# A chunked recurrence on one core: products per head and a dense state instead of products per head pair

## The chip, the cores and the metric
The kernel runs on one core of a Trainium2 chip. The metric is device time in microseconds (us) of one execution. Three runs of the kernel before took 1755.32, 1756.28 and 1759.92 us (median 1756.28). The profile is one further execution; its own time and its span stand below.

## The reference, cut to what matters
The program computes two blocks in float32, for 512 tokens of width 1024. The first block has a mixer whose left half is a recurrence over tokens in 8 heads of width 64, and whose right half is a causal convolution of 31 taps followed by a layer norm over 512 channels:

```
def step(S, inp):
    r_t, w_t, k_t, v_t, a_t, b_t = inp
    sa = jnp.einsum("bhvk,bhk->bhv", S, a_t)
    S = S * w_t[:, :, None, :] + sa[..., None] * b_t[:, :, None, :] + v_t[..., None] * k_t[:, :, None, :]
    y = jnp.einsum("bhvk,bhk->bhv", S, r_t)
    return S, y
...
y = _head_group_norm(y, lnx_g, lnx_b)
...
c = jax.nn.silu(_layer_norm(_causal_dwconv(c, cconv_w, cconv_b), cln_g, cln_b))
mix = jnp.concatenate([rwkv_out, c], axis=-1) @ w_out
```

The initial S is zero. The rest of the first block (a gated feed-forward with a short convolution) and the second block (two attention layers with modulation vectors from `silu(c) @ ada_w + ada_b`) are not touched.

## The kernel before, in words
Activations lie transposed, channels on the 128 partitions and tokens along the free dimension. 512 channels of the recurrence are 4 tiles (`CT`) of 128, each with two heads: head e of a pair has partitions 64e to 64e+63. Large products run as three products of split values (`w_hi`, `w_lo`); GpSimd (POOL) makes the split of each 1 MB weight block in `split`, 4 quarters of two operations. One instruction queue per engine is written out by hand, in order; engines meet by semaphores, and all loads are issued in order by SyncE (SP).

The recurrence has three stages.

1. The units, before about 304 us. For each pair c and head e, `unit` on TensorE, ScalarE (ACT) and VectorE (DVE) inverts a triangular matrix per chunk of 64 tokens and makes from it `eA` (step W), `U` (step U), `RBt` and the part `ky` of the output that needs no state. In the same stage ACT and POOL compute most of the convolution's taps: ACT writes a scaled tap to one of four buffers, POOL adds it to `cacc` (line 670, 96 additions), and `conv_done` counts them. Two of those buffers lie where `SA` and the second state buffer lie.
2. The chain over 8 chunks (`for n in range(NCH)`, TensorE lines 918 to 965, DVE lines 2328 on). The state `St` holds a 128x128 matrix for each pair, with zeros in the two blocks off the diagonal; DVE clears both buffers first (line 2322), after it has waited for the last tap. A chunk is: the products `eA` times state (line 926) for SA; `SA = product + U` on DVE (line 2332); the products of the state with `eR` (line 933); the products of B with SA and of K with V for the next state, 64x128 operands (lines 939, 940); per head SA with `RBt` (line 944) for the output; on DVE the old state times its decay (line 2337, two operations), then eight operations that add the product times the decay to the diagonal blocks (line 2345); and the output added to `ky` (line 2363).
 Beside the chunks stand: the products of the modulation vectors, one 1 MB block of `ada_w` after chunks 0, 2, 3, 5 and 6 (`CHAIN_ADA`, line 771, each 32 products); the convolution's mean in four 128x512 products after chunk 1 (line 950), centring on DVE (line 2351), squares on ACT, their sum in 32-partition blocks after chunk 4 (line 958), the root on ACT, its reciprocal on DVE and its spreading after chunk 5 (line 964), and the normalization on DVE (line 2361).
3. The group norm of `ky` (line 991 on), gating on POOL (line 682), and the output projection (lines 977 to 979), whose first tiles take the convolution's half.

SP's order in this stretch: two blocks of `ada_w`; the first output weight block once TensorE has read modulation block 0; the second once it has read block 1; then the third after the first is split; then further `ada_w` and weight blocks. POOL's order: additions of taps; splits of output blocks 0, 1 and 2; gating of the bonus (line 678); gating by `ky` (line 682); split of block 3.

Of the kernel before, what the change touches and what calls it, by code (L numbers as in the profile page):

```python
# [23 lines left out]
P = 128  # L24
# [90 lines left out]
def build(nc, x_t, ctx_t, stream, ada_w, vectors, squares, level_masks, scan_mask, ropes, lora_w, gate_w,  # L115
# [92 lines left out]
    St = [reg("St0", [P, CT, P], 143), reg("St1", [P, CT, P], 90)]  # L208
# [71 lines left out]
    ACT_STEPS = ["LT", "DIT", "MV", "Y0", "G1", "G2", "G3", "G4", "G5", "W", "U"]  # L280
    DVE_STEPS = ["MT", "RB", "RK", "DT0", "D0"] + [s + str(n) for n in range(1, 5) for s in "PT"] + ["Q5"]
# [14 lines left out]
    st_zero = sem("st_zero")  # L296
# [136 lines left out]
    kpe_copied = Later(sa_full, NCH)  # L433
    kpe_turned = Later(sa_done, NCH)
# [3 lines left out]
    mla_filled = Later(st_done, 2 * (NCH - 1))  # L438
# [49 lines left out]
    lam_exp = Later(cln_root, 3)  # L488
# [48 lines left out]
    def _(sp):  # L537
# [40 lines left out]
        ada_block(4, 2)  # L578
        weights(out0 + 3, out0 + 4)
        ada_block(5, 3)  # L580
        sp.wait_ge(y_done, NCH)
        sp.wait_ge(cln_sum, 1 + CT)
# [51 lines left out]
    def _(pool):  # L634
# [40 lines left out]
        split(out0 + 2, half_of(out0 + 2), out0 // 2 + 1, done=out0, to=0, hi=w3_hi, lo=w3_lo)  # L675
# [3 lines left out]
        for c in range(CT):  # L679
            pool.wait_ge(gn_centred, c + 1)  # L680
            pool.wait_ge(*bonus_gated.at(c + 1))
            pool.tensor_tensor(gg[:, c, :], gg[:, c, :], ky[:, c, :], ALU.mult).then_inc(y_gated.sem, 1)
        split(out0 + 3, half_of(out0 + 3), (out0 + 3) // 2, done=out0, to=0, hi=w4_hi, lo=w4_lo)
# [35 lines left out]
    def _(pe):  # L719
# [195 lines left out]
        CHAIN_ADA = {0: 1, 2: 2, 3: 3, 5: 4, 6: 5}  # L915
        pe.wait_ge(st_zero, 1)
        for e in range(2):
            pe.wait_ge(u_act[e], act_at(CT - 1, "U"))
        for n in range(NCH):
            tt, r = n // 2, slice(64 * (n % 2), 64 * (n % 2) + 64)  # L920
            t0 = CHUNK * n
            state = St[n % 2]
            if n:
                pe.wait_ge(st_done, 2 * n)
            for c in range(CT):
                mm = pe.matmul(banks[0][r, P * c:P * c + P], eA[:, c, t0:t0 + CHUNK], state[:, c, :], start=True, stop=True)
            mm.then_inc(sa_full, 1)
            if n >= 2:
                pe.wait_ge(y_done, n - 1)
            yb = banks[2 + n % 2]  # L930

            for c in range(CT):
                pe.matmul(yb[:, CHUNK * c:CHUNK * c + CHUNK], state[:, c, :], eR[:, c, t0:t0 + CHUNK], start=(c == 0), stop=False,
                          skip_group_check=True)
            pe.wait_ge(sa_done, n + 1)
            if n < NCH - 1:
                for c in range(CT):
                    ch = slice(P * c, P * c + P)
                    pe.matmul(banks[1][:, ch], B_tok[r, tt, ch], SA[r, ch], start=(c == 0), stop=False, skip_group_check=True)
                    mm = pe.matmul(banks[1][:, ch], K_tok[r, tt, ch], V_tok[r, tt, ch], start=False, stop=(c == CT - 1), skip_group_check=True)  # L940
                mm.then_inc(st_full, 1)
            for h in range(8):
                c, hr = h // 2, slice(64 * (h % 2), 64 * (h % 2) + 64)
                mm = pe.matmul(yb[hr, CHUNK * c:CHUNK * c + CHUNK], SA[r, 64 * h:64 * h + 64],
                               RBt[h][r, tt, 64 * (n % 2):64 * (n % 2) + 64], start=False, stop=(h == 7), skip_group_check=True)
            mm.then_inc(y_full, 1)
            if n == 1:
                pe.wait_ge(conv_done, len(ADDED))
# [1174 lines left out]
    def _(dve):  # L2123
# [197 lines left out]
        for st in St:  # L2321
            last = dve.memset(st[:, :, :], 0.0)
# [799 lines left out]
```

## Time and profile before
| | |
|---|---|
| median of 3 runs | 1756.28 us |
| the profiled execution's own time | 1760.59 us |
| its span | 1758.8 us |
| TensorE busy | 1679.9 us (96%) |
| VectorE / ScalarE / GpSimd busy | 1008.4 / 759.2 / 953.3 us |

### The profile page before, as it was taken

The numbers are of one execution on the slowest core, as the hardware profiler recorded it, in microseconds if no ns is written. First come the engines' busy times: TensorE is split into PE (matmuls) and PEld (weight loads), VectorE is DVE, ScalarE is ACT, GpSimd is POOL, SyncE is SP. The second block draws the span as 40 slices with busy tenths as digits, with TensorE's granted clock in tenths as the row PEclk, the third lists the DMA queues.
The fourth block names the chain that finished last, engine by engine and source line by source line (L and its number), as shares of the span: only waits on it lengthen the run. The fifth ranks groups of instructions, "written<-read, shape, count | busy, mean of one in ns | idle before, by whom it ended". The sixth has DMA issues, their size and how long they took to land.

```text
span 1758.8 us, 26144 instructions
## 1 busy us (share of the span) xinstructions
PE 1679.9 (96%) x10282; PEld 1368.5 (78%) x10282; DVE 1008.4 (57%) x1276; ACT 759.2 (43%) x1253; POOL 953.3 (54%) x758
## 2 busy tenths in 40 slices
PE   8999999988899999998998999999989999999887
PEld 7677998766588888887887777776877888888775
DVE  4698564574655555003346566676575666666575
ACT  4552888022333333003223655656134444444562
POOL 4444899734399999998446032034634444444062
PEclk9999999699899999999999999999989999999998
DMA  5221000433022222434112000002231111111211
GB/s 193 72 96 48 2 1 18 177 121 120 25 95 95 95 95 95 168 113 163 49 48 72 1 25 15 11 0 77 91 157 49 49 48 49 48 49 48 92 53 48
DMA packets 18867, 126.33 MB, mean 72 GB/s; under 512 B 2096, under 2 KB 2352, under 8 KB 4304
## 3 DMA queue, kind: packets, MB, share of 16 engines
q1 hardware_dynamic: 18624, 124.41, 19.3%
q8 instruction: 72, 1.18, 0.3%
q10 hardware_dynamic: 144, 0.52, 0.1%
q14 instruction: 27, 0.22, 0.0%
HBM read 122.83 MB, written 2.10 MB: 71 GB/s over the span
## 4 chain that ended last, share of the span: by engine, by line
PE 53%; issue 18%; POOL 16%; DVE 9%; ACT 3%; DMA 0%; POOLq 0%; ACTq 0%; DVEq 0%; SPq 0%
POOL w_hi L648 8%; PE banks L1227 5%; POOL cacc L670 4%; PE banks L1206 4%; POOL w_lo L639 3%; PE banks L1384 3%; PE banks L1387 3%; PE banks L1385 3%; PE banks L1089 3%; PE banks L1094 3%; PE banks L1090 3%; PE banks L751 2%; PE banks L1439 2%; PE banks L752 2%; PE banks L753 2%
## 5 line engine op out<-in xcount | busy, mean ns | idle before, releaser
L648 POOL TENSOR_TENSOR w_hi<-raw,der 128x512 fp32r<-128x512 f32 x296 | 340.8, 1162 | 454.4 <-PE banks L1387 186.9
L639 POOL TENSOR_TENSOR w_lo<-raw,w_hi 128x512 fp32r<-128x512 f32 x336 | 468.5, 1406 | 66.2 <-ACT w_hi L1530 66.2
L751 PE MATMUL banks<-h_hi,w_hi 128*128 128x512 f32 x496 | 198.5, 400 | 5.6 <-DVE h_lo L2369 5.3
L752 PE MATMUL banks<-h_lo,w_hi 128*128 128x512 f32 x496 | 194.1, 391 | 0.0
L753 PE MATMUL banks<-h_hi,w_lo 128*128 128x512 f32 x496 | 193.9, 391 | 0.0
L1384 PE MATMUL banks<-h_hi,w_hi 128*128 128x512 f32 (+1 forms) x384 | 146.4, 381 | 1.2 <-DVE h_lo L2685 1.0
L1385 PE MATMUL banks<-h_lo,w_hi 128*128 128x512 f32 (+1 forms) x384 | 131.5, 357 | 2.3 <-issue 2.3
L2014 ACT ACTIVATE dP<-banks,der 128x768 f32<-128x768 f32 x64 | 57.7, 902 | 160.2 <-DVE der L2773 160.2
L751 PEld LDWEIGHTS banks<-h_hi,w_hi 128*128 128x128 f32 x496 | 93.5, 188 | 35.2 <-issue 12.7
L1387 PE MATMUL banks<-h_hi,w_lo 128*128 128x512 f32 (+1 forms) x384 | 116.4, 357 | 0.0
L698 POOL TENSOR_TENSOR Of<-Of,Ls 128x768 f32<-128x768 f32 x8 | 14.7, 1832 | 186.7 <-DVE Ls L2575 186.7
L752 PEld LDWEIGHTS banks<-h_lo,w_hi 128*128 128x128 f32 x496 | 93.7, 189 | 19.9 <-issue 1.4
L753 PEld LDWEIGHTS banks<-h_hi,w_lo 128*128 128x128 f32 x496 | 93.7, 189 | 19.7
L2773 DVE TENSOR_REDUCE der<-banks 128x1 f32<-128x768 f32 x64 | 60.7, 953 | 68.3 <-PE banks L1420 68.3
L1227 PE MATMUL banks<-Pf,V 128*128 128x512 f32 x192 | 98.9, 596 | 0.3 <-issue 0.3
L1089 PE MATMUL banks<-h_hi,w_hi 128*128 128x512 f32 (+1 forms) x256 | 92.0, 359 | 5.1 <-DVE h_lo L2472 2.3
L2564 DVE TENSOR_REDUCE nmr<-banks 128x1 fp32r<-128x768 f32 x64 | 60.5, 945 | 59.7 <-PE banks L1177 58.9
L1867 ACT ACTIVATE Pf<-banks 128x512 f32<-128x512 f32 x112 | 66.6, 595 | 62.7 <-PE banks L1206 60.9
L1384 PEld LDWEIGHTS banks<-h_hi,w_hi 128*128 128x128 f32 x384 | 72.7, 189 | 18.1 <-DVE h_lo L2685 2.3
L1090 PE MATMUL banks<-h_lo,w_hi 128*128 128x512 f32 (+1 forms) x256 | 85.3, 350 | 0.0
L1385 PEld LDWEIGHTS banks<-h_lo,w_hi 128*128 128x128 f32 x384 | 73.0, 190 | 13.0 <-issue 4.7
L670 POOL TENSOR_TENSOR cacc<-glu_s,cacc 128x512 f32<-128x512 f32 x48 | 60.6, 1286 | 34.5 <-ACT glu_s L1628 34.5
(490 smaller groups left out, 4095.8 us busy)
## 6 DMA issues: line engine op xcount, KB each, us to landing
raw<-in_stream SPq DMA_DIRECT2D x84, 1024.0 KB, 4.8
ada_raw<-in_ada_w SPq DMA_DIRECT2D x18, 1024.0 KB, 7.0
raw<-in_ada_w SPq DMA_DIRECT2D x4, 1024.0 KB, 5.0
xT<-in_x_t SPq DMA_DIRECT2D x2, 1024.0 KB, 6.0
xT<-in_x_t SPq DMA_DIRECT2D x1, 2048.0 KB, 7.7
ada_end<-in_ada_w SPq DMA_DIRECT2D x2, 1024.0 KB, 6.0
out_t<-z SPq DMA_DIRECT2D x8, 256.0 KB, 2.1
ctxT<-in_ctx_t SPq DMA_DIRECT2D x1, 1024.0 KB, 7.2
```

The lines of the kernel that those rows point to most:

```text
L639: return pool.tensor_tensor(lo[:, h, part(i), :], raw_tiles(half)[:, part(i), :], hi[:, h, part(i), :], ALU.subtract)
L648: pool.tensor_tensor(hi[:, h, part(i), :], raw_tiles(half)[:, part(i), :], one, ALU.mult).then_inc(hi_done, 1)
L670: pool.tensor_tensor(cacc[:, j, :], tap_out[i % 4], cacc[:, j, :], ALU.add).then_inc(conv_done, 1)
L751: pe.matmul(banks[b][:, :], hi, tile(rhs_hi, k), start=(at_k == 0), stop=False)
L752: pe.matmul(banks[b][:, :], hi, tile(rhs_lo, k), start=False, stop=False)
L753: mm = pe.matmul(banks[b][:, :], lo, tile(rhs_hi, k), start=False, stop=(at_k == KT - 1))
L1089: pe.matmul(out, hi, cols(rhs_hi, k0 + k, a, b), start=(k == 0), stop=False)
L1090: pe.matmul(out, hi, cols(rhs_lo, k0 + k, a, b), start=False, stop=False)
L1227: mm = pe.matmul(pairs[1][:, 0, :], v[:, j, :], Pf[:, i % 4, :], start=(j == 0), stop=(j == 5), skip_group_check=True)
L1384: pe.matmul(out, hi, h2_hi[:, k, a:b], start=(k == 0), stop=False)
L1385: pe.matmul(out, hi, h2_lo[:, k, a:b], start=False, stop=False)
L1387: mm = pe.matmul(out, lo, h2_hi[:, k, a:b], start=False, stop=(k == KT - 1))
```

## The change
- The state becomes dense: two buffers `state` of 128 x 4 x 64 without the zero blocks, and all products of the chain are made per head with 64x64 operands, the two heads of a pair in different rows or columns of TensorE.
- The decay of a chunk is put into `eA` and `eR` in the units: on DVE, step W (which was on ACT) multiplies while it copies, and one more operation per pair scales `eR`. The old state times its decay goes to ACT (`keep_state`, four operations of 128x64 for each chunk from 1 to 6, into `kept`), and DVE then makes the next state in one addition of 128x256.
- Chunk 0 has no products with the state: SA is `U`, the next state is a copy, the buffers are not cleared, and the wait for the last tap stands before SA of chunk 1.
- The mean of the convolution is summed in 32-partition blocks (`conv_sums`) and spread (`conv_spread`), as the squares were; the pieces of that layer norm are placed one by one behind SA and behind the output in DVE's order. ACT loads the square root's table before the chain.
- Output accumulates in one bank per head half and is added in two operations of 64x256. Modulation block 1 stands behind chunk 1. POOL splits output block 2 after the gatings instead of before them; SP loads `ada` block 5 before output block 3.

```
-            for c in range(CT):
-                mm = pe.matmul(banks[0][r, P * c:P * c + P], eA[:, c, t0:t0 + CHUNK], state[:, c, :], start=True, stop=True)
+                for c, e, h, cc_ in HEADS:
+                    mm = pe.matmul(pairs[SA_PAIR][r, e, cc_], eA[HEAD[e], c, ts], kv[HEAD[e], c, :], start=True, stop=True)
...
+                for c, e, h, cc_ in HEADS:
+                    pe.matmul(banks[STATE_BANK][HEAD[e], cc_], K_tok[r, tt, h], V_tok[r, tt, h], start=(c == 0), stop=False, skip_group_check=True)
+            if n:
+                pe.wait_ge(y_done, n)
+                for c, e, h, cc_ in HEADS:
+                    mm = pe.matmul(banks[Y_BANK[e]][HEAD[e], cc_], kv[HEAD[e], c, :], eR[HEAD[e], c, ts], start=(c == 0), stop=False, skip_group_check=True)
+                mm.then_inc(y_begun.sem, 1)
+                if n == 1:
+                    pe.wait_ge(conv_done, len(ADDED))
+                    conv_sums(cacc)
+                if n == 2:
+                    conv_spread(1)
+                if n == 6:
+                    conv_spread(4)
+                pe.wait_ge(sa_done, n)
+            if n < NCH - 1:
+                for c, e, h, cc_ in HEADS:
+                    mm = pe.matmul(banks[STATE_BANK][HEAD[e], cc_], B_tok[r, tt, h], sa[r, h], start=False, stop=(c == CT - 1), skip_group_check=True)
+                mm.then_inc(st_full, 1)
+            for c, e, h, cc_ in HEADS:
+                mm = pe.matmul(banks[Y_BANK[e]][HEAD[e], cc_], sa[r, h], RBt[2 * c + e][r, tt, 64 * (n % 2):64 * (n % 2) + 64],
+                               start=(n == 0 and c == 0), stop=(c == CT - 1), skip_group_check=True)
             mm.then_inc(y_full, 1)
...
+        def keep_state(n):
+            act.wait_ge(st_done, n)
+            for c in range(CT):
+                ins = act.activation(kept[:, c, :], state[n % 2][:, c, :], ACT.Copy, scale=der[:, ECT + NCH * c + n:ECT + NCH * c + n + 1])
+            ins.then_inc(state_kept, 1)
...
+            if step == "W":
+                if e:
+                    decayed(eR[:, c, :], eR[:, c, :], slice(0, P))
+                dve.wait_ge(u_pe[e], pe_at(c, "W"))
+                decayed(eA[HEAD[e], c, :], X[0][HEAD[e], :], HEAD[e]).then_inc(u_dve[e], 1)
...
-                for e in range(2):
-                    hr = slice(64 * e, 64 * e + 64)
-                    for c in range(CT):
-                        ins = dve.scalar_tensor_tensor(out=kept, in0=banks[1][hr, P * c + 64 * e:P * c + 64 * e + 64], ...)
+                if n:
+                    dve.wait_ge(state_kept, n)
+                    dve.tensor_tensor(after, banks[STATE_BANK][:, 0:256], kept[:, :, :].rearrange("p c v -> p (c v)"), ALU.add).then_inc(st_done, 1)
+                else:
+                    dve.tensor_copy(after, banks[STATE_BANK][:, 0:256]).then_inc(st_done, 1)
```

Behind SA, DVE centres tiles 1 and 3 in chunks 3 and 4, adds modulation columns in chunk 5, normalizes tile 0 in chunk 6 and tiles 2 and 3 in chunk 7; behind the output it centres tiles 0 and 2 in chunks 2 and 3, adds modulation columns in chunk 4, inverts the root in chunk 5 and normalizes tile 1 in chunk 6. ACT's queue has squares of the centred tiles between `keep_state(2)` and `keep_state(5)`, each behind DVE's centring.

## Rows read from the trace of the kernel before

**Rows 1.** Page, part 1: busy time, share of span and instructions by engine.
```profile
PE 1679.9 (96%) x10282; PEld 1368.5 (78%) x10282; DVE 1008.4 (57%) x1276; ACT 759.2 (43%) x1253; POOL 953.3 (54%) x758
```

**Rows 2.** Windows: stretch, its length, busy by engine, PEclk, DMA share, GB/s.
```profile
176.00:304.00 128.00, 126.47 (x1159) 120.34 (x1161) 73.12 (x112) 105.55 (x184) 115.52 (x94) 1.00 0.01 2
...
308.80:319.20 10.40, 10.40 (x112) 9.45 (x112) 3.85 (x16) 0.00 (x0) 4.73 (x5) 0.50 0.48 200
319.20:333.70 14.50, 14.50 (x60) 10.14 (x56) 5.71 (x14) 0.00 (x0) 13.78 (x13) 0.54 0.43 146
...
308.80:373.56 64.76, 59.10 (x736) 49.91 (x737) 37.95 (x104) 9.43 (x14) 32.60 (x28) 0.79 0.31 114
```

**Rows 3.** Chain of waits, 300 to 382 us: start, length, what.
```profile
306.28 1.27 POOL cacc L670
...
308.80 1.97 PE banks L926 x8
...
327.84 5.96 PE banks L950 x8
...
373.56 5.33 PE banks L991 x8
```

**Rows 4.** Timeline, 290 to 345 us, TensorE: start, length, engine, line, operands.
```profile
303.88 0.94 PEld L771 LDWEIGHTS banks<-raw,sq_c 128*32 128x32 f32 x64
...
316.30 0.93 PEld L944 LDWEIGHTS banks<-RBt,SA 64*64 64x64 f32 x16 [0.22 <-issue]
316.31 1.12 PE L944 MATMUL banks<-RBt,SA 64*64 64x64 f32 x16
...
317.35 1.69 PEld L771 LDWEIGHTS banks<-raw,sq_c 128*32 128x32 f32 x64
...
337.77 0.54 PEld L944 LDWEIGHTS banks<-RBt,SA 64*64 64x64 f32 x16
```

**Rows 5.** Timeline, 345 to 402 us, TensorE.
```profile
353.20 0.81 PEld L958 LDWEIGHTS banks<-csq,sq_c 128*32 128x32 f32 x32
...
361.64 0.97 PEld L964 LDWEIGHTS banks<-crs,der 128*128 128x128 f32 x8 [1.45 <-DVE crs L2357]
```

**Rows 6.** Groups by line, 308.80 to 373.56 us: busy, mean ns, idle before.
```profile
L2345 DVE SCALAR_TENSOR_TENSOR St<-banks,der,St 64x64 f32<-64x64 f32 x56 | 12.3, 281 | 12.4 <-PE banks L940 12.0
...
L2332 DVE TENSOR_TENSOR SA<-banks,U 64x512 f32<-64x512 f32 x8 | 5.5, 688 | 12.8 <-PE banks L926 12.7
...
L2363 DVE TENSOR_TENSOR Q<-banks,Q 128x256 f32<-128x256 f32 x8 | 3.4, 421 | 0.9 <-PE banks L944 0.8
...
L2351 DVE SCALAR_TENSOR_TENSOR cacc<-banks,cacc 128x512 f32<-128x512 f32 x4 | 2.5, 682 | 0.0
...
L2357 DVE RECIPROCAL crs<-crs 128x128 f32<-128x128 f32 x1 | 1.0, 953 | 0.0
...
L1680 ACT ACTIVATE crs<-banks,der 128x128 f32<-128x128 f32 x1 | 0.4, 367 | 10.1 <-PE banks L958 10.1
```

**Rows 7.** Timeline, 264 to 280 us, DVE between two pairs of units.
```profile
274.07 1.29 DVE L2284 TENSOR_TENSOR Gt<-banks,sq_c 128x512 f32<-128x512 f32 x2 [5.30 <-PE banks L904]
```

**Rows 8.** Timeline, POOL and SP: first and second output block, third block's load.
```profile
314.47 2.04 POOL L648 TENSOR_TENSOR w_hi<-raw,der 128x512 fp32r<-128x512 f32 x2 [6.92 <-DMA raw<-in_stream]
...
323.61 0.33 SPq L547 DMA_DIRECT2D raw<-in_stream  x1
```

**Rows 9.** Timeline, 386 to 462 us, POOL.
```profile
404.34 2.22 POOL L648 TENSOR_TENSOR w_hi<-raw,der 128x512 fp32r<-128x512 f32 x2 [11.86 <-PE banks L979]
```

**Rows 10.** Timeline, 386 to 470 us, DVE: beside POOL's split, and without.
```profile
389.82 1.51 DVE L2394 TENSOR_TENSOR Q<-Q 128x512 f32<-128x512 f32 x1
...
394.33 0.69 DVE L2394 TENSOR_TENSOR Q<-Q 128x512 f32<-128x512 f32 x1
```

**Rows 11.** Line 944 alone: shortest, median, longest ns of one instruction.
```profile
L944 PE MATMUL banks<-RBt,SA x128: 218/218/363, 316.3 to 372.8; 64*64 64x64 f32 x128
```

**Rows 12.** DMA issues, whole execution: count, KB each, median us to landing.
```profile
ada_raw<-in_ada_w SPq DMA_DIRECT2D x18, 1024.0 KB, 7.0
```

More of the change, by code:

```diff
@@ L207, in build @@
     SA = reg("SA", [P, HALF], 88)
-    St = [reg("St0", [P, CT, P], 143), reg("St1", [P, CT, P], 90)]
+    state = [reg(f"state{i}", [P, CT, 64], 32 + i) for i in range(2)]
+    kept = reg("kept", [P, CT, 64], 34)
     sqk = reg("sqk", [P, 2, T], 101)
@@ L914, in _, with conv_sums @@
         ada_blocks([0])
-        CHAIN_ADA = {0: 1, 2: 2, 3: 3, 5: 4, 6: 5}
-        pe.wait_ge(st_zero, 1)
+        CHAIN_ADA = {1: 1, 2: 2, 3: 3, 5: 4, 6: 5}
         for e in range(2):
             pe.wait_ge(u_act[e], act_at(CT - 1, "U"))
+            pe.wait_ge(u_dve[e], dve_at(CT - 1, "W"))
+        def conv_sums(src):
+            for c in range(CT):
+                for j in range(4):
+                    mm = pe.matmul(banks[CONV_BANK][32 * j:32 * j + 32, 0:P], ones[:, 0:32], src[:, c, P * j:P * j + P], start=(c == 0),
+                                   stop=(c == CT - 1))
+            mm.then_inc(cln_sum, 1)
@@ L919, in _, with conv_spread @@
+        def conv_spread(done):
+            pe.wait_ge(cln_root, done)
+            for j in range(4):
+                mm = pe.matmul(banks[CONV_BANK][:, P * j:P * j + P], der[:, ROOT + j:ROOT + j + 1].broadcast_to([P, P]), crs[:, :], start=True, stop=True)
+            mm.then_inc(cln_root, 1)
+        HEADS = [(c, e, slice(64 * (2 * c + e), 64 * (2 * c + e) + 64), slice(64 * c, 64 * c + 64)) for c in range(CT) for e in range(2)]
         for n in range(NCH):
-            tt, r = n // 2, slice(64 * (n % 2), 64 * (n % 2) + 64)
@@ L942, in _ @@
[L942 to L945, printed above, removed]
-            mm.then_inc(y_full, 1)
-            if n == 1:
-                pe.wait_ge(conv_done, len(ADDED))
-                for c in range(CT):
-                    mm = pe.matmul(banks[4][:, :], ones, cacc[:, c, :], start=(c == 0), stop=(c == CT - 1))
-                mm.then_inc(cln_sum, 1)
+                pe.wait_ge(st_done, n)
@@ L954, in _ @@
             if n == 4:
[L955 to L965 removed]
+                pe.wait_ge(cln_sq, CT)
+                conv_sums(csq)
         pe.wait_ge(y_done, NCH)
@@ L1654, in unit @@
                 out, src = Gt[e][:, :, :], X[0][:, :]
-            elif step == "W":
-                out, src = eA[rows, c, :], X[0][rows, :]
             else:
@@ L2319, in _ @@
                     unit(c, e, step)
-        dve.wait_ge(conv_done, len(ADDED))
-        for st in St:
-            last = dve.memset(st[:, :, :], 0.0)
-        last.then_inc(st_zero, 1)
         chain.link(dve.memset(der[:, ROOT:ROOT + 4], 0.0))
@@ new lines, in norm_conv, with by_head, behind_sa @@
+        def norm_conv(c):
+            dve.wait_ge(cln_root, 5)
+            dve.tensor_tensor(cacc[:, c, :], cacc[:, c, :], banks[CONV_BANK][:, :], ALU.mult).then_inc(cln_normed, 1)
+        def by_head(t):
+            return t.rearrange("p (c e v) -> p e c v", c=CT, e=2)
+        def behind_sa(n):
+            if n == 3:
+                centre_conv(1)
+            elif n == 4:
+                centre_conv(3)
+            elif n == 5:
+                ada_columns(1)
+            elif n == 6:
+                norm_conv(0)
+            elif n == 7:
+                norm_conv(2)
+                norm_conv(3)
@@ L2368, in low @@
+            dve.wait_ge(y_full, n + 1)
+            for e in range(2):
+                ins = dve.tensor_tensor(ky[HEAD[e], :, ts], banks[Y_BANK[e]][HEAD[e], 0:256].rearrange("p (c t) -> p c t", c=CT),
+                                        ky[HEAD[e], :, ts], ALU.add)
+            ins.then_inc(y_done, 1)
+            behind_y(n)
         def low(k, src, ready):
```

149 lines of the change are left out of this document (75 added, 74 removed).

## The prediction
> **What bounds the kernel now.** I read the page's busy times first, then the windows around the change, then the chain of waits in them, then the timeline. TensorE is busy for 96% of the span [rows 1], so time leaves mainly where it has nothing better to do. The recurrence's chain is such a place: 308.80 to 373.56 us, 64.8 us, and no engine is at its peak in it [rows 2]. The chain of waits runs there through POOL's last tap (ends 307.55), then the small matmuls from 308.80, the convolution's mean (5.96 us) and DVE, until the group norm's first product at 373.56 [rows 3]. Three things make it long. The granted clock is 0.50 in 308.8 to 319.2 and 0.54 in 319.2 to 333.7, so at the 1.2 GHz level for nearly 25 of the 65 us, though TensorE is recorded busy throughout [rows 2]. Operands are twice as wide as needed. And DVE makes the next state in eight operations of 281 ns [rows 6]. The units in front (176 to 304 us) are another matter: TensorE is busy 126.5 of 128 us [rows 2].
>
> **The units.** DVE gets, per pair, two operations from the bank (64x512, priced as line 2332: 0.69 us) and one of 128x512 (as line 2351: 0.68) [rows 6]: 2.06 us. DVE idles 5.30 us at just that place, between the last placement of one pair and the first product of the next [rows 7]. Cost 0. Bounds: if the broadcast factor doubled them to 4.1 us they would still fit; without the cover four pairs would cost 8 us. ACT loses two copies per pair, and TensorE, the bound, waited for neither: gain 0, at most 1 us. POOL's taps keep their pace.
>
> **Where the chain starts.** Before, DVE waits for the last tap, clears two buffers, and TensorE starts at 308.80. After, chunk 0 needs neither: TensorE goes on behind modulation block 0, whose weight loads run 303.88 to 304.82, and begins at about 305.0 [rows 3, 4]. Gain 3.8 us; the tap's end at 307.55 meets chunk 1's SA, which comes no earlier than 308.
>
> **The price of a group.** All products are now like line 944: 8 heads, 16 instructions of 64x64. Its loads take 0.93 us at the low clock and 0.54 at the high one; the last result is 0.19 behind [rows 4]. Different row/column placements are not shown in the trace; I bound a group by 0.3 us (half, if neighbours in different quarters overlap more) and, above, by 16 times the 218 ns that one instruction lasts [rows 11], 3.5 us, and take the row itself, since its placement is that of three of the five groups. The tiling page of the Trainium skill (TensorEngine Tiling (Array Packing), "Key Properties") says that different tiles can load and multiply in parallel; at a quarter of the price each the groups would be worth some 20 us more than I count, but line 944 already alternates tiles and shows its price.
>
> **One chunk.** There are five groups: SA, K with V, state with eR, B with SA, SA with RBt.
> - Low clock: 5 x 0.93 = 4.65 us. TensorE is the longer side: SA's addition (0.69) lies beside two groups, and the state's addition (0.42, as line 2363 [rows 6]) beside the last.
> - High clock: three groups 1.62; the fourth 0.54 + 0.14; the state 0.42 and two handovers 0.12; sum 2.84. SA on DVE (0.69) starts after the output's two additions of the chunk before (2 x 0.42; the two ends meet at 0.9 us into the chunk) and ends at 1.6, just in time.
> - ACT's four copies per chunk at about 0.3 to 0.37 each (line 1680 reads 128x128 in 0.37 [rows 6]) make 1.2 to 1.5 us, beside 2.4 us of path. In chunks 3 and 4 they stand behind a square of 0.6 that waits for DVE's centring: 0.3 us lost each. If these copies took twice as long, six chunks would lose 0.5 to 1 each; hence 5 us in the upper end.
>
> **What stands beside the chunks.** A modulation block takes 0.94 us high and 1.69 low [rows 4], as before in five chunks; it is paid after the last group, less what DVE has to do there. Sums in 32-partition blocks take 0.81 high [rows 5], I take 1.6 low. They replace the mean of 5.96 us. Spreading takes 0.97 high [rows 5] and 1.8 low, now twice instead of once. Behind the output DVE has the inverse of 0.95 and a centring of 0.68 [rows 6]; behind SA a piece of 0.68 is hidden by the fourth group.
>
> **The sum.** The clock decides, and no row shows it for this sequence. Before, small products at the low level for 19 us did not raise it, the dense 128x512 mean was followed by the high one, and small products after that mostly kept it [rows 2, 3, 4]. The change enters at the high level and without the pause of 3.8 us, but with emptier operands and no dense stretch. I take the low level for chunks 0 to 3 and the high one for 4 to 7, near the middle:
> chunk 0: three groups, 2.8; chunk 1: 4.65 + 1.6 + 1.7 = 7.95; chunk 2: 4.65 + 1.8 + 1.7 = 8.15; chunk 3: 4.65 + 1.7 = 6.35; chunk 4: 2.84 + 0.3 + 0.85 = 4.0; chunk 5: 2.84 + 0.8 (columns) + 0.95 = 4.6, the block beside it; chunk 6: spreading 0.4 beyond SA's addition, block 0.95, normalizing 0.6: 4.75; chunk 7: SA 0.68 + 0.75, two normalizations 1.36, output 0.96: 3.75. Together 42.3; the chain ends at 305.0 + 42.3 = 347.3 instead of 373.56: 26.2 us earlier.
>
> **What is late next.** POOL: output block 0 lands at 314.47 and is split until 323.6 as before, when SP issues block 2 [rows 8]; block 1 follows until about 333, the bonus until 338.5. All is before 347. Splitting block 2 now comes after the gatings: about 347.3 + 8.6 to + 18.5, block 3 to + 28. TensorE turns to block 2's tiles where POOL in the old trace found block 0's weights released, 404.34, so + 30.8 [rows 9]. Covered by 12 us; without cover 10 us. Loads: SP issues `ada` blocks 4 and 5 behind output block 2 (323.6); with the median landing of 7.0 us [rows 12] they are there at about 331 and 335, and chunks 5 and 6 want them at 339 and 344. At the high clock throughout they would be late. Group norm and projection follow the chain and move with it. But POOL's split now runs on beside DVE's last gatings: an operation that takes 0.69 alone took 1.51 beside POOL [rows 10]. Five of them, with slack in three: 1 us, bounds 0 and 3.
>
> Net 25.2 us. The profiled execution's own time is 1760.59 (span 1758.8, with 1.8 around it); 1760.59 - 25.2 = 1735.4. The median of the runs is 4.3 lower, 1756.28, so I say 1731.
>
> **Rivals.**
> 1. The clock stays high from start to end. Chunk 0 then takes 1.7 instead of 2.8, chunks 1 to 3 12.9 instead of 22.45 (2.84 each, 1.6 for the sums and spreading beyond SA's addition, blocks and centring), 10.6 less. But chunk 5 asks for its modulation block at 326 and it lands at 331, so 5 go back: end at 341.7, net 30.8, time 1725. For it: no pause before the chain. Against: the drop to 0.50 at 308.8, and TensorE recorded busy at that level until 327.8 [rows 2, 3]. The Trainium skill (TensorE: Matmul & The Clock Gate, "What's actually happening") says that activity releases the throttle; by it this is the case to expect, but the trace disagrees as far as busy time counts as activity: 10.4 of 10.4 us busy at 0.50.
> 2. The clock stays low to the end. Chunks 4 to 7 take 6.4, 6.35, 8.15 and 4.3 instead of 17.1: 8.1 more, net 17, time 1739. For it: quarter-filled products, and nothing dense any more.
> 3. The chain shortens but the gain is handed back behind it: the projection waits for POOL's later split, or for loads that SP holds back. It needs both covers above to fail, 12 us and more: net 10 or less, time 1748.
> 4. Slower: the 64x64 groups do not overlap. If two heads in the same bank or quarter had to wait for each other, an instruction would cost up to its own 218 ns [rows 11]. There are 36 groups x 16 = 576; my sum counts some 45 ns of pace each. Break-even is 25.2 us over 576, 44 ns more, so a pace of about 90 ns; at 218 ns the chain is 100 us longer. At 130, midway: + 49, less 25: 1780. Against it: line 944 runs at 34 to 58 ns a piece with alternating output halves.
> That the change doesn't do what it says I see no room for: each old group is gone from the text.
>
> **Chances.** Forecast (1731, own range 1727 to 1736) 0.46; all low 0.25; all high 0.17; handed back 0.08; slower 0.04. The range must reach the first two rivals and the copies on ACT: 1721 to 1745. A measurement of this kernel tells 0.3%, 5 us, from no change. Faster 0.93, same 0.03, slower 0.04.
>
> **What would show it.** After: line 2332's successor 0.69 us, the new state one operation of 0.42, SA groups at 0.54 or 0.93; the granted clock per chunk decides between forecast and rivals 1 and 2. TensorE's first chain product right behind modulation block 0 at about 305; the group norm's first product at 347, and from there to the first projection tile still 8.6 us. Unit stage still 128 us. I am wrong if a group takes over 1 us at the high clock, if ACT's copies end after the fourth group, or if TensorE idles before block 2's tiles.

## The result and the profile after

| | before | after |
|---|---|---|
| median of the runs | 1756.32 us (1755.32 to 1759.92) | 1732.66 us (1730.67 to 1739.2) |
| ratio, 95% interval | | 0.9868 [0.9838, 0.9898] |
| profiled execution's own time | 1760.59 us | 1731.96 us |
| its span | 1758.8 us | 1730.2 us |
| group norm's first product | 373.56 us | 344.78 us |
| first projection tile | 382.21 us | 353.49 us |
| end of the convolution's half of the projection | 429.22 us | 401.18 us |

The forecast was 1731. The two traces differ by 28.6 us, the medians by 23.7. The first trace of before was an execution 4.3 us above its median, and a second trace of the same kernel (run before_again, 1758.14) has the group norm at 372.5 instead of 373.56. There the chain also begins 2.6 us later than in the first trace (311.42 for 308.80), so it lasts 61.1 us against 64.8. In the traces of all versions below, what follows the end of the convolution's half lasts 1326.7 to 1332.2 us, though the code is the same there. What follows therefore reads places and lengths from traces and the size of a gain from medians.

Part 1 of the page after, which answers to [rows 1]: TensorE is busy 28.9 us less, about the whole of the gain in the trace.
```profile
PE 1651.0 (95%) x10522; PEld 1345.9 (78%) x10522; DVE 1004.5 (58%) x1230; ACT 760.9 (44%) x1271; POOL 958.0 (55%) x758
```

The windows of the changed kernel, with the columns of [rows 2]: the unit stage, chunks 1 and 2, chunk 5, chunk 6, the group norm, and last the whole chain.
```profile
176.00:303.50 127.50, 125.96 (x1148) 119.96 (x1145) 82.14 (x128) 100.08 (x175) 118.01 (x94) 1.00 0.01 2
...
306.20:312.10 5.90, 4.91 (x176) 4.37 (x176) 2.81 (x6) 5.27 (x15) 0.99 (x1) 1.00 0.99 407
312.10:317.30 5.20, 4.97 (x159) 4.47 (x152) 1.95 (x4) 0.00 (x0) 2.04 (x3) 1.00 0.87 320
...
325.70:334.80 9.10, 4.61 (x148) 4.21 (x144) 5.77 (x9) 2.85 (x7) 9.10 (x9) 0.83 0.89 349
334.80:341.20 6.40, 6.40 (x156) 6.00 (x152) 2.58 (x6) 0.81 (x1) 3.22 (x3) 0.71 0.37 150
...
344.78:353.49 8.71, 7.84 (x16) 2.45 (x16) 6.51 (x9) 5.69 (x10) 5.90 (x5) 0.80 0.89 346
...
304.54:344.78 40.24, 31.87 (x983) 28.87 (x977) 23.56 (x44) 17.88 (x43) 25.26 (x22) 0.92 0.57 214
```
The chain takes 40.24 us against 64.76. The clock column is the surprise: 1.00 where [rows 2] had 0.50 and 0.54, and then a fall of its own in chunks 5 and 6. Chunk 5 shows why: 9.10 us long, with TensorE busy for only 4.61 of them.

The chain of waits of the changed kernel (start, length, what) names what stood there.
```profile
305.01 10.18 DMA raw<-in_stream
...
324.62 8.20 DMA ada_raw<-in_ada_w
...
332.96 1.93 PE banks L775 x64
...
344.78 5.40 PE banks L1004 x8
```
Where [rows 3] had the convolution's mean on the path, it now goes through two loads: an output weight block, whose split (begun at 315.26) lets SP issue the next blocks, then modulation block 4, issued at 324.6. The timeline of the changed kernel shows the same place from TensorE's side, with the chain's first group and, last, POOL's split of output block 4.
```profile
304.54 0.54 PEld L949 LDWEIGHTS banks<-V_tok,K_tok 64*64 64x64 f32 x16
...
324.62 1.56 SPq L557 DMA_DIRECT2D ada_raw<-in_ada_w  x2
...
332.93 1.72 PEld L775 LDWEIGHTS banks<-ada_raw,sq_c 128*32 128x32 f32 x64 [3.67 <-issue]
332.96 1.93 PE L775 MATMUL banks<-ada_raw,sq_c 128*32 128x64 f32 x64 [3.56 <-DMA ada_raw<-in_ada_w]
...
376.31 2.22 POOL L652 TENSOR_TENSOR w_hi<-raw,der 128x512 fp32r<-128x512 f32 x2 [0.76 <-PE banks L992]
```
TensorE stands for 3.56 us, and after that the weight loads of this block take 1.72 us instead of the 0.94 of [rows 4]. Before, the landings of 7.0 us [rows 12] were hidden.

The groups by line in the chain of the changed kernel (mean ns of one, then idle before), which answer to [rows 6]:
```profile
L1691 ACT ACTIVATE kept<-state,der 128x64 f32<-128x64 f32 x24 | 6.3, 335 | 4.6 <-DVE state L2425 4.6
...
L2417 DVE TENSOR_TENSOR SA<-banks,U 64x512 f32<-64x512 f32 x7 | 4.8, 690 | 6.6 <-PE banks L945 6.1 <-POOL cacc L674 0.2
...
L2425 DVE TENSOR_TENSOR state<-banks,kept 128x256 f32<-128x256 f32 x6 | 2.5, 425 | 5.0 <-PE banks L966 4.9
...
L2430 DVE TENSOR_TENSOR Q<-banks,Q 64x256 f32<-64x256 f32 x16 | 6.7, 421 | 0.8 <-PE banks L971 0.5
```
Eight additions of 281 ns are one of 425, and the last tap (POOL, line 674) costs SA only 0.2 us.

### The profile page after: what moved, and what is told of

The parts are those of the page before. It is cut to its first block, busy times and chain, and to the rows that moved or that the text cites. A ratio compares the mean times of both kernels' runs of the same rounds, so it can differ in the third digit from the quotient of the medians.

```text
span 1730.2 us, 26591 instructions
## 1 busy us (share of the span) xinstructions
PE 1651.0 (95%) x10522; PEld 1345.9 (78%) x10522; DVE 1004.5 (58%) x1230; ACT 760.9 (44%) x1271; POOL 958.0 (55%) x758
## 4 chain that ended last, share of the span: by engine, by line
PE 56%; issue 16%; POOL 12%; DVE 9%; ACT 5%; DMA 1%; POOLq 0%; SPq 0%; ACTq 0%; DVEq 0%
POOL w_hi L652 9%; PE banks L1240 5%; PE banks L903 4%; POOL w_lo L643 4%; PE banks L1219 4%; PE banks L1397 3%; PE banks L1400 3%; PE banks L1398 3%; PE banks L1102 3%; PE banks L1107 3%; PE banks L1103 3%; PE banks L755 2%; PE banks L1452 2%; PE banks L756 2%; PE banks L757 2%
```

## The experiments

"Changed kernel" is the one after. Each is compared with before on its own chip; kernels of one set share their runs of before. The first theory: the changed chain ran at the high clock because it begins without a pause, and a large part of what that brought went back in the wait for modulation block 4 and the clock's fall behind it. Three sets follow. All differences are between medians, unless a trace is named.

### The first set: clock, load, state addition

**again**: the changed kernel once more, as the yardstick of this set.

> The changed kernel once more, unaltered, so that its profiled execution can be compared with its timed runs. Theory: the change is worth what the chain of the recurrence lost, 28.8 us in the two traces (group norm's first product at 344.78 instead of 373.56), and the median of the runs differs by less (23.7 us) because the executions differ in the clock they are granted in the chain. Then the median lies at 1731 to 1734 and the trace again starts the group norm at 343 to 348. Rival: some us are given back behind the chain in the timed runs; then the trace would show the group norm at 345 but a span above 1735.

Measured: 1730.68 (1730.4 to 1735.9), 0.9853 [0.9834, 0.9872]. Group norm at 344.7, a wait of 2.86 us for the same block: the chain's length, the wait and the fall behind it are confirmed. The clock's course is not the same, though. Windows of again:
```profile
316.00:320.00 4.00, 3.12 (x102) 2.88 (x103) 1.55 (x4) 0.90 (x3) 4.00 (x5) 0.74 0.15 59
320.00:324.00 4.00, 4.00 (x143) 3.84 (x142) 3.23 (x6) 1.32 (x4) 4.00 (x4) 0.84 0.02 4
```
It is at the low level from 318 to 321 as well, behind a halt of 1.33 us in TensorE's issue that ends at 316.88 and that was 0.23 us long in the first trace. The fourth chunk ends 1.9 us later than there, and the wait for the load takes most of that in.

**load_first**: SP issues modulation blocks 4 and 5 before the third output weight block.
```
         weights_behind(out0 + 1, 1)
-        weights(out0 + 2, out0 + 3)
         ada_block(4, 2)
         ada_block(5, 3)
+        weights(out0 + 2, out0 + 3)
```

> Modulation blocks 4 and 5 are loaded before output block 2 instead of behind it. Theory: TensorE's wait of 3.56 us at 329.4 to 332.96 is for a load that stood in the queue behind another, and the fall of the granted clock right after it (0.71 in 334.8 to 341.2) is a result of the wait. Then both go: block 4 is there before 325, the chain ends at 338 to 340 instead of 344.8, and the time falls by 5 to 6 us against the changed kernel. Rival: the low clock comes from the small products themselves; then only the wait goes, 2.5 to 3.5 us (VectorE's reciprocal ends at 331.9), and the clock falls in the same stretch.

Measured: 1726.36 (1726.2 to 1729.8), 0.9825 [0.9808, 0.9842], 4.3 less than again. Group norm at 340.5, 4.2 earlier. Windows of load_first, columns as above:
```profile
325.00:331.00 6.00, 6.00 (x152) 5.42 (x148) 3.91 (x8) 1.43 (x5) 6.00 (x7) 0.72 0.66 251
331.00:340.50 9.50, 7.76 (x269) 6.91 (x265) 8.64 (x16) 5.32 (x9) 7.88 (x7) 1.00 0.34 114
340.50:347.60 7.10, 6.19 (x17) 1.90 (x17) 6.45 (x10) 5.67 (x10) 4.93 (x4) 1.00 0.86 328
```
No wait for a load is left. The clock still falls once, from 326 to 329, behind a gap of 1.58 us in TensorE's issue that begins at 323.1, but it is at 1.00 in the group norm, which takes 7.1 us instead of 8.71. So the load did cost what the trace showed at that place. The gain of 4.3 lies between the 5 to 6 of the theory and the 2.5 to 3.5 of its rival: the fall behind the load is gone, another one is there. By its median this is the fastest version of all.

**pause_back**: TensorE waits before chunk 0 until DVE has waited for the last tap and cleared two buffers, as in the kernel before.
```
+        pe.wait_ge(prep_done, 3)
...
+        dve.wait_ge(conv_done, len(ADDED))
+        for i in range(2):
+            last = dve.memset(state[i % 2][:, :, :], 0.0)
+        last.then_inc(prep_done, 1)
```

> The changed kernel with the former start: VectorE waits for the last tap, clears both state buffers, and only then TensorE begins chunk 0, after a pause of about 3.5 us. Theory of the prediction: the pause puts the clock at the low level and small products alone hold it there for chunks 0 to 3, so it costs 3.5 us and another 8 to 10, less what the later wait for the modulation block swallows (that wait vanishes): chain end 350 to 353, 6 to 9 us slower. Rival: 64x64 products raise the clock within some us as they did at 339 in the changed kernel; then the loads' wait swallows most and the chain ends at 345 to 348, 0 to 4 us slower.

Measured: 1735.46 (1733.89 to 1744.79), 0.9887 [0.9856, 0.9917], 4.8 more than again. Group norm at 347.2, as the rival said. Windows of pause_back: the pause, what follows, and the rest of the chain in two parts.
```profile
303.50:308.01 4.51, 1.14 (x65) 0.97 (x65) 0.61 (x4) 4.31 (x7) 2.48 (x2) 0.97 0.64 225
308.01:314.80 6.79, 6.79 (x128) 6.43 (x128) 2.14 (x7) 1.06 (x4) 0.00 (x0) 0.52 0.79 327
314.80:334.60 19.80, 17.25 (x592) 15.70 (x584) 12.99 (x25) 8.18 (x24) 19.27 (x18) 1.00 0.57 218
334.60:347.20 12.60, 9.39 (x269) 8.37 (x265) 7.98 (x16) 5.37 (x9) 3.49 (x3) 0.86 0.21 83
```
The pause brings the low level back, but for less than 7 us, in which stand six groups of 64x64 products and the start of the convolution's sums. Before, after a pause of the same length, it stayed at 0.50 to 0.54 for some 24 us [rows 2]. So the pause explains the fall and not the length of what follows. The group norm is only 2.5 later than in again, with a chain that begins 3.5 later: part of the delay falls into time that the load's wait took before. The first projection tile is 0.8 later and the end of the convolution's half 0.6. So most of the 4.8 us lies behind all that the pause touches directly: between the two traces it arises after 790 us, mostly just before 1277, and its cause is not known.

**eight**: the new state in eight additions of 64x64 instead of one of 128x256.
```
-                    dve.tensor_tensor(after, banks[STATE_BANK][:, 0:256], kept[:, :, :].rearrange("p c v -> p (c v)"), ALU.add).then_inc(st_done, 1)
+                    for e in range(2):
+                        for c in range(CT):
+                            ins = dve.tensor_tensor(state[(n + 1) % 2][HEAD[e], c, :], banks[STATE_BANK][HEAD[e], 64 * c:64 * c + 64],
+                                                    kept[HEAD[e], c, :], ALU.add)
+                    ins.then_inc(st_done, 1)
```

> The next state is added in eight operations of 64x64 on VectorE instead of one of 128x256, all else as changed. Theory: the state's addition is on the path in every chunk, eight of 0.28 with overlap took 1.79 us before against 0.42 now, so six chunks lengthen by 1.2 to 1.4 us each, less what modulation blocks on TensorE (0.94 us behind the last group) cover in chunks 1, 2, 3, 5 and 6 and what the wait for the load swallows: 2 to 5 us slower, chain end 347 to 350. Rival: TensorE is the longer side in every chunk and nothing changes, chain end 345.

Measured: 1733.62 (1729.51 to 1739.84), 0.9869 [0.9841, 0.9897]. Each addition takes 218 ns, 1.74 a chunk instead of 0.42, yet the group norm is at 345.8, only 1.1 later than in again and not at the 347 to 350 that was expected, and the wait for the load still stands at 3.53. The intervals of again and eight overlap. A trap for a reader of single edits: with a fixed landing time in the chain, what is added ahead of it is swallowed, so this run says little of what one addition is worth without it.

### The second set: the same question, from the kernel before

**before_again**: the kernel before, unaltered.

> The kernel before, unaltered, for a second trace. Its first trace is of an execution 4.3 us over the median, with the low clock from 308.8 to 333. Theory: how long the clock stays low after the pause differs from execution to execution, and an execution near the median has it low for some 8 us less, so that the group norm starts 3 to 5 us earlier (369 to 371). Rival: the low stretch is the same, the group norm starts at 373.5 again, and the difference lies elsewhere.

Measured: 1757.61 (1755.36 to 1758.58), 0.9988 [0.9974, 1.0001]. Windows of before_again:
```profile
308.80:324.00 15.20, 12.58 (x121) 11.29 (x122) 4.99 (x20) 1.85 (x4) 8.17 (x9) 0.56 0.54 216
324.00:340.00 16.00, 15.06 (x176) 11.72 (x176) 12.64 (x30) 2.05 (x4) 15.64 (x14) 0.99 0.43 158
340.00:350.00 10.00, 9.18 (x115) 8.44 (x116) 6.33 (x15) 1.65 (x2) 10.00 (x9) 0.66 0.53 197
```
The clock's course differs from execution to execution. Here it is low for some 14 us, from 310.2, and for 24 us in [rows 2]; the chain starts low after the pause in both. The chain is 3.7 us shorter, but begins later, so the group norm is not at the 369 to 371 of the theory. Two more things can be read. The level rises at 324.1 in the small products of chunk 1, before the dense mean at 327.57. And it falls again at 341.4, behind 1.45 us of waiting for SA, and with the same wide products it is back after less than 7 us.

**before_filled**: four idle 128x512 products into an unused bank in the pause ahead of the chain.
```
         CHAIN_ADA = {0: 1, 2: 2, 3: 3, 5: 4, 6: 5}
+        for _ in range(4):
+            pe.matmul(banks[3][:, :], ones, A_tok[:, 0, :], start=True, stop=True)
         pe.wait_ge(st_zero, 1)
```

> The kernel before with four added 128x512 products on TensorE in its pause before the chain (305 to 308.8; they write a bank that nobody reads). Theory: the pause is what costs the clock; filled, the chain starts high, its first 19 us of products shrink by 6 to 9 us, and the kernel is 5 to 9 us faster. Rival: wide small products at the chain's density cannot hold the high level, the clock falls within a few us after the start, and the time is that of before.

Measured: 1753.66 (1745.1 to 1756.97), 0.9965 [0.9949, 0.9982]. The median is 4.0 less than before_again's, under the 5 to 9 of the theory, and hides two groups: three of its ten runs are at 1745 and seven at 1751 to 1757. The profiled one is one of the three (1745.12); its windows:
```profile
304.00:308.90 4.90, 4.70 (x73) 2.34 (x73) 1.01 (x4) 4.06 (x7) 3.30 (x3) 1.00 0.73 252
308.90:330.00 21.10, 20.42 (x287) 16.62 (x287) 16.05 (x43) 0.01 (x1) 15.57 (x14) 1.00 0.52 197
330.00:361.90 31.90, 26.24 (x453) 23.14 (x451) 24.46 (x62) 9.46 (x14) 17.93 (x15) 1.00 0.28 99
361.90:368.90 7.00, 6.13 (x17) 1.84 (x17) 6.32 (x10) 4.40 (x7) 5.09 (x4) 1.00 0.86 330
```
With nothing of the chain changed, the clock stays at 1.00 to its end, the group norm is at 361.9 and the first projection tile at 368.9, 13.3 us before the 382.21 of the first trace. That execution is 12.5 us faster than the median of before_again. The slower seven have no trace, but each run's mean granted clock is on record: 0.986 to 0.988 for the three fast ones, 0.977 to 0.980 for the seven, 0.974 to 0.980 for the kernel before in the same set. So the seven lost the clock somewhere although the pause was filled; where is not shown.

**before_heads**: in the kernel before, only the products of B with SA and of K with V are made per head, 64x64, in the place of 64x128.
```
-                for c in range(CT):
-                    ch = slice(P * c, P * c + P)
-                    pe.matmul(banks[1][:, ch], B_tok[r, tt, ch], SA[r, ch], start=(c == 0), stop=False, skip_group_check=True)
-                    mm = pe.matmul(banks[1][:, ch], K_tok[r, tt, ch], V_tok[r, tt, ch], start=False, stop=(c == CT - 1), skip_group_check=True)
+                for h in range(8):
+                    hr, ch = slice(64 * (h % 2), 64 * (h % 2) + 64), slice(64 * h, 64 * h + 64)
+                    pe.matmul(banks[1][hr, ch], B_tok[r, tt, ch], SA[r, ch], start=(h < 2), stop=False, skip_group_check=True)
+                    mm = pe.matmul(banks[1][hr, ch], K_tok[r, tt, ch], V_tok[r, tt, ch], start=False, stop=(h > 5), skip_group_check=True)
```

> The kernel before with the products for the next state (B with SA, K with V) made per head with 64x64 operands instead of 64x128; all else as before. Theory of the prediction: two groups of 16 at 0.93 (low) or 0.54 (high) take the place of 16 instructions in 3.84 or 1.93 us, so a chunk loses 2.0 us at the low clock and 0.85 at the high one, less what VectorE's decay of the old state then leaves uncovered: 5 to 8 us faster, group norm at 366 to 369. Rival: the state's decay on VectorE (0.84 to 2.4 us behind SA) is the longer side in most chunks and only 0 to 3 us are gained.

Measured: 1750.92 (1749.41 to 1753.01), 0.9958 [0.9942, 0.9974], 6.7 less than before_again. The chain lasts 56.6 us (309.13 to 365.7) against 61.1. Its window behind the pause:
```profile
308.80:318.50 9.70, 9.37 (x132) 8.63 (x133) 4.14 (x18) 0.00 (x0) 3.51 (x4) 0.51 0.53 223
```
The low stretch is some 10 us here, and another one of 10 us follows at 346, so the clock is no better than in before_again and the shorter groups must carry the gain: narrower operands in two of the five groups are worth some 7 us.

**best**: load_first, and the last two normalizations and a set of modulation columns moved to later places in DVE's order, to take them out of the last chunk.
```
+            if 4 + c == CONV_BANK:
+                pe.wait_ge(cln_normed, CT)
...
-            elif n == 5:
-                ada_columns(1)
             elif n == 6:
+                ada_columns(1)
                 norm_conv(0)
-            elif n == 7:
-                norm_conv(2)
-                norm_conv(3)
...
+            elif n == 7:
+                norm_conv(2)
+                norm_conv(3)
```

> The changed kernel with modulation blocks 4 and 5 loaded before output block 2, the second set of modulation columns moved from behind SA of chunk 5 to behind SA of chunk 6 (where VectorE waited for the spread root), and the last two normalizations of the convolution moved from before to behind the output of chunk 7, beside the group norm's first product. Theory: 0.8 us in chunk 5 and 1.3 us in chunk 7 come on top of the loads' 4.3 us: group norm at 338 to 339 and 1724 to 1725 us. Rival: the last normalizations then hold up TensorE's second group norm product and the convolution's half of the projection, and nothing is gained beyond the loads' order, 1726.

Measured: 1732.89 (1725.93 to 1735.04), 0.9845 [0.9824, 0.9866]: the expectation of 1724 to 1725 fell; one run of five, 1725.93, came near it. One 128x8 addition on DVE, all of whose operands are in SBUF, took 5.67 us. Timeline of best, DVE and then POOL:
```profile
334.76 5.67 DVE L2243 TENSOR_TENSOR ada<-ada_col,prm 128x8 f32<-128x8 f32 x1
...
335.47 4.95 POOL L681 TENSOR_TENSOR Q<-Q,gg 128x512 f32<-128x512 f32 x4
```
It ends at 340.43, POOL's four gatings at 340.42. TensorE waits 3.96 us for the state behind it, its clock falls, and the group norm is at 345.8, in a chain that begins at 307.02, 1.9 later than in load_first.

### The third set: the 128x8 addition, and POOL's order

**load_cols**: load_first, and only the second set of columns moved, behind the chain.
```
-            elif n == 5:
-                ada_columns(1)
...
+        ada_columns(1)
         ada_columns(2)
```

> Blocks 4 and 5 loaded before output block 2 (as load_first), and the second set of modulation columns moved from behind SA of chunk 5 to behind the whole chain. Theory: in chunk 5 the next state then waits for its product alone, 0.8 us earlier than before, and behind the chain VectorE has 0.5 to 0.7 us more ahead of the first centring, beside TensorE's group norm product: group norm at 339.5 to 340, time 1725.5 to 1726.5 against 1726.4 of load_first. Rival: the additional work behind the chain delays centring by as much, 1726.4 to 1727.

Measured: 1731.32 (1728.24 to 1738.22), 0.9841 [0.9823, 0.9859], above the expected 1725.5 to 1727. The profiled execution is its slowest, and it was the first set, not moved, that ran into POOL. Timeline of load_cols, DVE and then POOL:
```profile
328.16 11.05 DVE L2241 TENSOR_TENSOR ada<-ada_col,prm 128x8 f32<-128x8 f32 x1
...
331.82 2.50 POOL L643 TENSOR_TENSOR w_lo<-raw,w_hi 128x512 fp32r<-128x512 f32 x2
334.26 4.94 POOL L681 TENSOR_TENSOR Q<-Q,gg 128x512 f32<-128x512 f32 x4
```
DVE ends at 339.21, POOL at 339.20, after splits and gatings without a gap, ten operations of it beside the one of DVE. The group norm is at 352.2. Eleven microseconds go to an addition of 1,024 numbers. As the row did not come in every execution, the spread of 10 us between runs has a candidate here.

**cols_six** and **cols_six_free**: load_first with the second set in chunk 6, without and with POOL's gatings held until the last output (`pool.wait_ge(y_done, NCH)` ahead of line 681).

> As load_first, with the second set of modulation columns behind SA of chunk 6. Theory of the lock: VectorE's addition of 128x8 with all operands in SBUF cannot run while POOL's four bonus gatings (128x512, 1.24 us each) follow each other without a gap, as in best, where it lasted 5.67 us and ended with POOL's last gating. Here too it lasts from SA of chunk 6 to the end of POOL's gating, 4 to 5.5 us, and the group norm starts at 344 to 346. Rival: the 5.67 us in best was an instruction fetch or chance; then it lasts 0.2 to 1.3 us as the others and the group norm starts at 340.

> As cols_six, and POOL starts its bonus gatings only after the last output of the chain. Theory of the lock: with POOL idle the 128x8 addition lasts 0.17 us and the group norm starts at 339 to 341; the gatings then end 5 us after it and delay what follows by 1 to 3 us. Rival: it is as long as in cols_six.

Measured: 1730.19 and 1730.12, two runs each. Timeline of cols_six:
```profile
338.57 2.10 DVE L2241 TENSOR_TENSOR ada<-ada_col,prm 128x8 f32<-128x8 f32 x1
```
It ends at 340.67, POOL's gatings at 340.64; group norm at 346.1. The 2.10 us are under the 4 to 5.5 expected, because chunk 6 came later. Timeline of cols_six_free:
```profile
334.40 0.17 DVE L2242 TENSOR_TENSOR ada<-ada_col,prm 128x8 f32<-128x8 f32 x1
...
341.14 0.95 DVE L2242 TENSOR_TENSOR ada<-ada_col,prm 128x8 f32<-128x8 f32 x1
...
340.79 5.42 POOL L682 TENSOR_TENSOR Q<-Q,gg 128x512 f32<-128x512 f32 x4 [6.40 <-DVE Q L2430]
```
With POOL idle the addition takes 0.17 us, and the group norm is at 340.7. Of these 5.4 us, 1.6 are a chain that begins earlier (305.48 for 307.08), 1.9 the addition, and 1.6 shorter halts in TensorE's issue. The gatings then come 5.1 us later, and at the end of the convolution's half the lead is 3.1 us; the rest goes behind it, at no place that was found. That POOL's work is what holds the addition is shown from both sides. How long it holds it is not: the next addition, at 341.14, runs beside the same gatings and takes only 0.95 us, to the end of the first of them. Two runs each can't tell the two versions apart, and a version that keeps both gains was not run.

**pool_order**: the changed kernel with POOL's split of output block 2 back ahead of the gatings.
```
             split(n, half_of(n), n // 2)
+        split(out0 + 2, half_of(out0 + 2), out0 // 2 + 1, done=out0, to=0, hi=w3_hi, lo=w3_lo)
         pool.wait_ge(*bonus_shifted.at(CT))
...
-        split(out0 + 2, half_of(out0 + 2), out0 // 2 + 1, done=out0, to=0, hi=w3_hi, lo=w3_lo)
```

> The changed kernel with POOL's split of output block 2 back in front of the gatings. Theory: block 2 is split 333 to 342.5, the bonus gatings run to 347.5, the gating by ky starts 0.5 to 1 us late and its last ends at the same distance; the split that the changed order has beside VectorE's last gatings is gone. So the same time within 1 us either way, 1730 to 1732. Rival: the gatings run beside VectorE's work of chunk 7 and the first centrings and hold its operations in SBUF; the chain or the first projection tile comes 2 to 4 us later.

Measured: 1734.63 (1734.25 to 1736.26), 0.9864 [0.9845, 0.9883]. That is 2.0 and 4.0 us more than the changed kernel's two medians, but before took 1758.93 in this set against 1756.32 and 1757.5, and the ratio lies between the two (0.9868 and 0.9853). Group norm at 344.0. The timeline of pool_order shows the same pair as best, in the group norm's first microseconds:
```profile
344.45 3.38 DVE L2241 TENSOR_TENSOR ada<-ada_col,prm 128x8 f32<-128x8 f32 x1
...
342.82 4.97 POOL L682 TENSOR_TENSOR Q<-Q,gg 128x512 f32<-128x512 f32 x4
```
The ends are 347.83 and 347.79. So the old order puts this addition beside POOL, but that it costs time in all is not shown. Neither does the later split gain anything that these runs can tell.

## Why the prediction was right, and where it was not

**Units: right.** 127.5 us as before [rows 2], though DVE has 9 us more busy time in them. The work costs 2 x 0.69 and 0.91 a pair, 0.23 more for the 128-partition one than I took, in the idle 5.30 us [rows 7].

**Start: right.** 304.54 for 305.0; the gain is 4.3 instead of 3.8, and the tap was no bound.

**Price of a group: right.** 0.54 at the high clock. An instruction on other rows and columns overlaps as in line 944, and rival 4 is out. The state's addition (0.425), SA (0.69), the output (2 x 0.42) and ACT's copies (0.335 each) are at their terms.

**Clock: wrong, and the mis-sized term.** I took the low level for chunks 0 to 3. It was at 1.00 until TensorE had waited 2.5 us for the block, to 331.9, so this part was rival 1 (in again it was low for 3.4 us of them). The chunks from the second on began at 306.22, 312.14, 317.32, 321.52, 325.70, 334.82 and 341.22, so they last 1.7, 5.9, 5.2, 4.2, 4.2, 9.1, 6.4 and 3.6 for 2.8, 7.95, 8.15, 6.35, 4.0, 4.6, 4.75 and 3.75. The first four are 8.3 us shorter than forecast. The row I held against it, 10.4 of 10.4 us busy at 0.50 [rows 2], was a row of what happens after a pause. pause_back and the trace of before_filled show that with the pause the chain starts low and without it high; the other seven runs of before_filled show that filling it is not enough. My reading that only the dense mean raised the level was of one trace: in before_again small products of chunk 1 were there when it rose. By the Trainium skill (TensorE: Matmul & The Clock Gate, "What's actually happening") activity releases the throttle. The traces agree that the level comes back after a stretch of work, but this stretch was 3.4 us long in load_first and 24 in the first trace of before, with TensorE recorded busy in most of it.

**Modulation block: wrong.** The landing at 331 was forecast well (332.8), but with low chunks it was to be wanted only at 339. With high ones it was wanted at 329.3, so the cover was gone, as rival 1 says. What rival 1 left out is the clock's fall in the wait: 0.50 from 332 to 338, and so 0.71 in chunk 6. Chunks 5 and 6 were 4.5 and 1.65 us longer than forecast, 6.1 together, and the chain's end at 344.78 came between rival 1's 341.7 and my 347.3. load_first takes the wait away and gets to 340.5. So 1731 was met in part by luck: the two errors have opposite signs. The step that failed is the clock of chunks 0 to 3, and with it the cover of modulation block 4.

**Behind the chain: right.** 8.71 us to the first tile for 8.6. From there to the end of the convolution's half 47.69 against 47.01, 0.7 for my 1. POOL had block 2 split at 363.4, 18.6 after the group norm, and block 3 at 375.5, 30.8 after it for my 28. It waited 0.76 us for TensorE at block 4 in place of 11.86 [rows 9], so little cover is left, but TensorE was busy for 43.57 of the 43.71 us behind the first tile; rival 3 is out.

**The sum.** Net 28.04 at the end of the convolution's half in the traces for 25.2. In medians 23.7 (again, in its set: 26.8 less than before's 1757.5). Not all of it is the new arithmetic: before_heads shows 6.7 us for operand width, before_filled up to 12.5 for the clock alone. They overlap and can't be added, and what the single addition of the state is worth was not isolated.

**Open.** Why the level stays low for 24, 14 and 10 us after the pause in traces of the old chain and for under 7 in pause_back was not settled. The operands' width alone is not it, since the same wide products had it back after less than 7 us from 341.4 in before_again. The halts with nothing shown as releaser have a pattern. Rows of the changed kernel, then of load_first and pause_back:
```profile
311.24 0.98 PE L775 MATMUL banks<-raw,sq_c 128*32 128x64 f32 x53 [0.97 <-issue]
...
324.66 0.50 PE L953 MATMUL banks<-eR,state 64*64 64x64 f32 x10 [1.58 <-issue]
...
333.68 0.57 PE L967 MATMUL banks<-SA,B_tok 64*64 64x64 f32 x13 [1.81 <-issue]
```
They stand at the same places of the program in every trace of the changed chain, 128 pairs of load and product apart, that is 256 instructions, and last from nothing to 1.81 us. The DMA view has a queue called "instruction" with packets of 0.02 MB; in the changed kernel they fall into the microseconds 309, 313, 316 and 321, and halts end at 311.2, 315.8, 319.5 and 323.3. That points to the loading of the program itself; why one halt is long and another short is not shown. That the slower executions of the changed kernel (1739.2) lose to the 128x8 addition was not seen in a trace of it: there it took 1.30, 1.01 and 0.17. On record is that their mean clock is lower: 0.977 at 1739.2 against 0.980 to 0.983 for the other three.

## What to carry to other kernels

When a chain gets shorter, list for each load on its way the time at which it will be wanted at the new pace, for the fastest clock you hold possible, and order the queue of loads by that; a swap of two load groups was worth 4.3 us here, after the change was made. Price the clock at both levels and ask what the engine did just before: behind a pause of 4 us the old chain ran at half the clock for 14 and 24 us in two traces. Follow a difference through the whole trace before you put a median down to one place, as the 4.8 us of pause_back show. And look behind each shift for small DVE operations whose operands are all in SBUF and which now fall beside uninterrupted work of POOL.

## What the hardware showed unexpectedly

- A DVE addition of 128x8 in SBUF takes 0.17 us alone. Beside POOL it ended, within 0.04 us, with the end of a POOL operation: with the one that ran when it began in ten cases of 0.66 to 1.30 us (changed kernel, load_first, best, cols_six, cols_six_free, pool_order), and with the last of POOL's whole run in four of 2.10, 3.38, 5.67 and 11.05 us. A pair of the first kind, from the changed kernel, where POOL goes on at 327.39:
```profile
326.17 1.28 POOL L643 TENSOR_TENSOR w_lo<-raw,w_hi 128x512 fp32r<-128x512 f32 x1
326.17 1.30 DVE L2241 TENSOR_TENSOR ada<-ada_col,prm 128x8 f32<-128x8 f32 x1
```
DVE operations with one operand in a bank in the same stretches kept their times (0.42, 0.69). The Trainium skill (SBUF — State Buffer, "Who interferes with whom") tells of a port pair that the two engines share, for which a DVE instruction with two inputs in SBUF contends with a GpSimd instruction that reads SBUF. The traces agree that they contend, and show that DVE can miss its turn between two of POOL's operations, through as many as ten of them. What decides whether it does is open.
- After a pause of under 4 us ahead of the chain the low level lasted under 7 us in pause_back, 10 in before_heads, and 14 and 24 in two executions of the kernel before.
- Four products of 3.7 us together, put into that pause, made three of ten executions some 12 us faster than the median of before_again, and the others by 0.6 to 6.3.
